# Sixteen gate tiles in pairs, each pair by seven products of 128 tokens, two couples of pairs ahead of two branch groups

## What is computed

```python
    y_a = dsa_attention(aq, ak, av, iq, ik, iw)
    y_b = dilated_attention(bq, bk, bv)
    y_m = memory_attention(mq.reshape(b, s, M_HEADS, M_HEAD_DIM), rmsnorm(mem, g_mem[l]), w_mem_kv[l])
    gates = jax.nn.sigmoid((n @ w_gate[l] + b_gate[l]).astype(jnp.float32)).astype(n.dtype)
    gates = gates.reshape(b, s, N_BRANCHES, d)
    merged = (gates[:, :, 0] * (y_a @ w_branch[l, 0])
              + gates[:, :, 1] * (y_b @ w_branch[l, 1])
              + gates[:, :, 2] * (y_m @ w_branch[l, 2]))
    h = h + merged @ w_out[l]
    h = h + hier_moe(rmsnorm(h, g_ffn[l]), w_group[l], b_group[l], w_sub[l], b_sub[l], w1[l], w3[l], w2[l])
```

## Time and profile before

| what | value |
|---|---|
| time, median of 3 runs | 1039.71 us (1039.53 to 1039.88) |
| profiled execution | 1039.46 us, its span 1037.6 us |
| PE busy | 1012.0 us (98%), 5196 matmul records |
| DVE busy | 445.2 us (43%) |
| ACT busy | 338.8 us (33%) |
| chain that ended last | PE 91%, DVE 4%, DMA 2%, ACT 1% |
| mean granted TensorE clock | 0.998 |

### The profile page before, as it was taken

How to read it: one execution, slowest core, us unless ns; L and a number is a source line. 1 busy time by engine, 2 the same in 40 slices (tenths; PEclk the granted TensorE clock), 3 DMA queues, 4 the chain that set the end, 5 groups by cost and what they waited for, 6 DMA issues and landing times.

```text
span 1037.6 us, 14005 instructions
## 1 busy us (share of the span) xinstructions
PE 1012.0 (98%) x5196; PEld 706.9 (68%) x5196; DVE 445.2 (43%) x1250; ACT 338.8 (33%) x803; POOL 65.2 (6%) x124
## 2 busy tenths in 40 slices
PE   6999999999999999999999999999999999999996
PEld 2468554547887777888888877888888844444442
DVE  5459836456356655355743424831012410000004
ACT  5224134335053247245553134730111411111112
POOL 0060000032100000000000000000000020000000
PEclk9999999999999999999999999999999999999999
DMA  9972125762243331444434342059536799999996
GB/s 362 420 300 84 41 81 197 291 243 81 82 148 136 122 122 63 170 169 151 158 134 155 131 194 81 2 216 422 213 138 227 277 381 422 420 422 419 422 420 253
DMA packets 33936, 227.49 MB, mean 219 GB/s; under 512 B 4577, under 2 KB 4849, under 8 KB 8112
## 3 DMA queue, kind: packets, MB, share of 16 engines
q1 hardware_dynamic: 30784, 214.97, 53.1%
q10 hardware_dynamic: 1920, 9.80, 2.5%
q0 software_dynamic: 1168, 1.85, 0.5%
HBM read 222.15 MB, written 8.41 MB: 222 GB/s over the span
## 4 chain that ended last, share of the span: by engine, by line
PE 91%; DVE 4%; DMA 2%; ACT 1%; issue 1%; SPq 0%; DVEq 0%; ACTq 0%
PE lin L580 21%; PE lin L1189 11%; PE sc L699 6%; PE aux L1189 5%; PE aux L580 5%; PE aux L1076 4%; PE sc L804 4%; PE lin L768 3%; PE aux L834 3%; PE sc L1154 3%; PE lin L820 3%; PE sc L580 3%; PE sc L983 2%; DVE UN L2004 2%; PE lin L596 2%; PE sc L596 2%
## 5 line engine op out<-in xcount | busy, mean ns | idle before, releaser
L580 PE MATMUL lin<-H,ring 128*128 128x256 f32 (+1 forms) x1008 | 222.5, 383 | 0.0
L580 PEld LDWEIGHTS lin<-H,ring 128*128 128x128 f32 x1008 | 191.4, 190 | 29.7 <-issue 4.2
L699 PE MATMUL sc<-H,ring 128*128 128x512 f32 (+1 forms) x192 | 67.3, 496 | 0.0
L2004 DVE SCALAR_TENSOR_TENSOR UN<-UN,cols 128x512 f32<-128x512 f32 (+1 forms) x120 | 66.7, 626 | 0.0
L1406 ACT ACTIVATE SP<-lin 128x512 f32<-128x512 f32 (+2 forms) x88 | 42.1, 486 | 72.1 <-PE lin L820 71.9
L1417 ACT ACTIVATE SP<-SP,ST 128x513 f32<-128x513 f32 (+4 forms) x88 | 53.9, 612 | 6.5 <-DVE ST L1919 6.2
L1916 DVE CUSTOM_DVE_ANT_0 SP<-sc,CW,SK 128x512 f32<-128x512 f32 (+1 forms) x48 | 31.8, 662 | 55.5 <-PE sc L804 55.5
L699 PEld LDWEIGHTS sc<-H,ring 128*128 128x128 f32 x192 | 34.8, 189 | 30.3 <-issue 25.6
L2411 DVE TENSOR_TENSOR PR<-lin,PR 128x512 f32<-128x512 f32 x8 | 5.5, 691 | 94.6 <-PE lin L1189 94.6
L804 PE MATMUL sc<-PR 64*128 64x256 f32 (+3 forms) x240 | 42.2, 434 | 2.9 <-DVE ST L1916 2.1
L1076 PE MATMUL aux<-Y,ring 128*128 128x256 f32 x192 | 42.2, 380 | 0.5 <-DVE Y L1928 0.5
(11 more groups left out here) (428 smaller groups left out, 1541.8 us busy)
## 6 DMA issues: line engine op xcount, KB each, us to landing
ring<-w_stream SPq DMA_DIRECT2D x119, 1024.0 KB, 5.2
SP<-w_stream SPq DMA_DIRECT2D x13, 1024.0 KB, 20.5
UN<-w_stream SPq DMA_DIRECT2D x10, 1024.0 KB, 19.3
PR<-w_stream SPq DMA_DIRECT2D x8, 1024.0 KB, 21.8
CW<-w_stream SPq DMA_DIRECT2D x8, 1024.0 KB, 21.8
X<-w_stream SPq DMA_DIRECT2D x8, 1024.0 KB, 23.8
Y<-w_stream SPq DMA_DIRECT2D x8, 1024.0 KB, 18.1
PR<-ada_in SPq DMA_DIRECT2D x5, 1024.0 KB, 26.8
```

The lines of the kernel that those rows point to most:

```text
L580: m = mm(dst, w[:, k, :], rhs(k), start=n == 0, stop=n == KT - 1)
L699: m = mm(bank[:, 0:ns * SEQ], filling["w"][:, k, :], H[:, 0:ns, k, :], start=k == 0, stop=k == KT - 1)
L2004: ins = v.scalar_tensor_tensor(out=CV[:, t, 0:ns, :], in0=u, scalar=w, in1=CV[:, t, 0:ns, :], op0=ALU.mult, op1=ALU.add)
```

## The change

The sixteen gate tiles that are made after the attention (8 to 23) are taken in eight pairs, two pairs are a couple (`GATES_LATE`), and the four couples go in twos: couples 0 and 1 ahead of branch groups `mp` 0 and 1, couples 2 and 3 ahead of `mp` 2 and 3. A pair is one ring unit `w` (two tiles, each split into two halves of the contraction, `lo` and `hi`). The tokens are split into two halves of 128 and the contraction into two halves; the product is made with seven products of four matmuls with 128 tokens. VectorE makes three sums of the weights beside one sum in place, and four sums of the tokens once. ScalarE copies partial results out of the bank between products that add to the same bank, VectorE adds the rest, and ScalarE then applies the sigmoid in SBUF. `MORE` and half of `X1` hold the weight sums, so SyncE loads nine expert units instead of eleven at the end of the attention, and four instead of two after the last branch product. The stream's order is changed to match, with the one block of padding moved behind the early gates.

```diff
+        G_S = [MORE[:, 512 * q:512 * (q + 1)] for q in range(4)] + [X1[:, 1024:1536], X1[:, 1536:2048]]
+        G_T = NB.rearrange("p (q k n) -> p q k n", q=4, k=4)
+        def gate_unit(c, x):
+
+            return FIRST_GATE + 2 * c + x + 3 * (c // 2)
...
+            def paired_gates(c):
...
+                for x in range(2):
...
+                    w[x] = unit_of_pair()
...
+                    if c:
+                        pe.wait_ge(quarter_added, g_added(c - 1, x, 3))
...
+                    quarter(g_banks(c, x)[0], w[x][:, 0, lo], h11).then_inc(quarter_made, 1)
+                for x in range(2):
+                    quarter(g_banks(c, x)[1], w[x][:, 0, hi], h21).then_inc(quarter_made, 1)
+                for x in range(2):
+                    pe.wait_ge(quarter_read, g_read(c, x, 1))
+                    pe.wait_ge(tokens_mixed, G_TOKENS + 3)
+                    pe.wait_ge(weights_mixed, G_WEIGHTS + 8 * c + 3 * (x + 1))
+                    quarter(g_banks(c, x)[0], G_S[x][1], t2, start=False).then_inc(quarter_made, 1)
...
             attention("abm", early_gate)
+            at["block"] += at["block"] % UNIT
+            turn["prefetch"] = at["block"] // UNIT + SLOTS
             for mp in range(4):
-                for n in range(max(EARLY, 6 * mp), 6 * mp + 6):
-                    gate(*divmod(n, 3))
+                if mp % 2 == 0:
+                    paired_gates(mp)
+                    paired_gates(mp + 1)
                 if mp == 0:
-                    turn["prefetch"] = at["block"] // UNIT + SLOTS
                     attended("abm")
...
-            for n in range(RING_AT - 2):
+            for n in range(RING_AT - 4):
                 sp.dma_start(ASIDE[n], w_stream[BASE + n].rearrange("p b n -> p (b n)")).then_inc(aside_in[n], 16)
...
-            for n in (RING_AT - 2, RING_AT - 1):
+            for n in range(RING_AT - 4, RING_AT):
                 load_expert(BASE + n, n)
...
+            def mixed_gate(c, x):
+
+                u, (lo, hi) = gate_unit(c, x), LO_HI
+                w, (s1, s2, s4) = ring[:, u % SLOTS, :, :], G_S[x]
+                dve.wait_ge(unit_in[u % SLOTS], 16 * (u // SLOTS + 1))
+                if c:
+                    dve.wait_ge(quarter_made, g_at(c - 1, x, 5))
+                v.tensor_tensor(s1, w[:, 1, lo], w[:, 1, hi], ALU.add).then_inc(weights_mixed, 1)
+                v.tensor_tensor(w[:, 1, lo], w[:, 0, lo], w[:, 1, lo], ALU.subtract).then_inc(weights_mixed, 1)
+                dve.wait_ge(weights_mixed, G_WEIGHTS + 8 * c + 3 * x + 1)
+                v.tensor_tensor(s2, s1, w[:, 0, lo], ALU.subtract).then_inc(weights_mixed, 1)
...
+            def mixed_first(p):
+
+                if p in (12, 14):
+                    mixed_gate(0, (p - 12) // 2)
+                elif p == 16:
+                    mixed_gate_last(0)
+
+            def joined_gates(c, then):
...
+                for x in range(2):
+                    to = halves_of(pairs[x][1])[1]
+                    dve.wait_ge(quarter_read, g_read(c, x, 7))
+                    v.tensor_tensor(to, to, G_Z[:, x, :], ALU.add).then_inc(quarter_added, 1)
+                    if x < len(then):
+                        mixed_gate(then[x], x)
+                for x in range(2):
...
+                    v.tensor_tensor(to, to, g_banks(c, x)[2], ALU.add).then_inc(quarter_added, 1)
+                if len(then) == 2:
+                    mixed_gate_last(then[0])
 
-            attention("abm")
+            attention("abm", mixed_first)
 
             for mp in range(4):
+                if mp % 2 == 0:
+                    joined_gates(mp, (mp + 1, mp + 1))
+                    joined_gates(mp + 1, () if mp else (2,))
                 for b in range(3):
...
+                if mp == 0:
+                    mixed_gate(2, 1)
+                    mixed_gate_last(2)
```

More of the change, by code:

```diff
@@ L101 @@
 FIRST_OUT = (4 + len(FIRST1) + sum(n if what == "gate" else 4 * n for what, _, _, n in SEQUENCE if what == "ada") + GATES) // 2
+FIRST_GATE = (4 + 14 + 4 * 8 + 6 + 2 * (KT + 2) + IN1 + IN2 + EARLY + 1) // 2
 FIRST_V = (4 + 14 + 4 * 8 + 6 + 2 * (KT + 2) + IN1 + BV) // 2
@@ L1050, in _ @@
             pe.wait_ge(idx_mask, 1)
-            def gate(t, b):
-                bank = lin_bank(("gate", t, b))
-                product(bank[:, 0:SEQ], lambda k: H[:, 0, k, :]).then_inc(lin_ready, 1)
+            def paired_gates(c):
+                lo, hi = LO_HI
+                h11, h12 = H[:, 0, 0:4, 0:P], H[:, 0, 0:4, P:SEQ]
+                h21, h22 = H[:, 0, 4:8, 0:P], H[:, 0, 4:8, P:SEQ]
+                t1, t3, t2, t4 = (G_T[:, q, :, :] for q in range(4))
+                w = {}
+                for x in range(2):
+                    assert at["block"] // UNIT == gate_unit(c, x)
+                    w[x] = unit_of_pair()
+                    if c == 0 and x == 0:
+                        pe.wait_ge(scores_taken, scored_first["abm"] + len(STAGES["abm"]))
+                        pe.wait_ge(fill_taken, GATES_FROM + EARLY)
+                        pe.wait_ge(lin_taken, at["lin"])
+                    if c:
+                        pe.wait_ge(quarter_added, g_added(c - 1, x, 3))
+                    if c >= 2:
+                        pe.wait_ge(quarter_read, g_read(c - 2, x, 4))
+                    quarter(g_banks(c, x)[0], w[x][:, 0, lo], h11).then_inc(quarter_made, 1)
[8 more added lines that the diff above has]
+                    if c:
+                        pe.wait_ge(quarter_read, g_read(c - 1, x, 4))
+                    quarter(g_banks(c, x)[2], G_S[x][0], t1).then_inc(quarter_made, 1)
+                for x in range(2):
+                    pe.wait_ge(quarter_read, g_read(c, x, 6))
+                    quarter(g_banks(c, x)[0], w[x][:, 1, lo], t3, start=False).then_inc(quarter_made, 1)
+                for x in range(2):
+                    pe.wait_ge(quarter_read, g_read(c, x, 5))
+                    pe.wait_ge(weights_mixed, G_WEIGHTS + 8 * c + 7 + x)
+                    quarter(g_banks(c, x)[2], G_S[x][2], h22, start=False).then_inc(quarter_made, 1)
+                for x in range(2):
+                    pe.wait_ge(quarter_read, g_read(c, x, 7))
+                    pe.wait_ge(tokens_mixed, G_TOKENS + 4)
+                    quarter(g_banks(c, x)[0], w[x][:, 1, hi], t4, start=False).then_inc(quarter_made, 1)
+                at["owed"] += 2
@@ L2197, in _ @@
                     v.tensor_tensor(BVT[:, 0, f1], BVT[:, 0, f1], gamma, ALU.add).then_inc(quarter_added, 1)
+                    if g == 1:
+                        g1, g3, g2, g4 = (G_T[:, q, :, :] for q in range(4))
+                        h11, h12, h21, h22 = (H[:, 0, k:k + 4, a:a + P] for k in (0, 4) for a in (0, P))
+                        v.tensor_tensor(g1, h12, h11, ALU.subtract).then_inc(tokens_mixed, 1)
+                        v.tensor_tensor(g3, h22, h12, ALU.subtract).then_inc(tokens_mixed, 1)
+                        dve.wait_ge(tokens_mixed, G_TOKENS + 1)
+                        v.tensor_tensor(g2, h22, g1, ALU.subtract).then_inc(tokens_mixed, 1)
+                        dve.wait_ge(tokens_mixed, G_TOKENS + 3)
+                        v.tensor_tensor(g4, h21, g2, ALU.subtract).then_inc(tokens_mixed, 1)
                 if t == BQ - 1:
@@ new lines, in mixed_gate_last @@
+            def mixed_gate_last(c):
+                for x in range(2):
+                    w, (s1, s2, s4) = ring[:, gate_unit(c, x) % SLOTS, :, :], G_S[x]
+                    dve.wait_ge(weights_mixed, G_WEIGHTS + 8 * c + 3 * x + 3)
+                    if c:
+                        dve.wait_ge(quarter_made, g_at(c - 1, x, 3))
+                    v.tensor_tensor(s4, w[:, 0, LO_HI[1]], s2, ALU.subtract).then_inc(weights_mixed, 1)
+            def mixed_first(p):
[3 more added lines that the diff above has]
+                    mixed_gate_last(0)
@@ L2236, in _ @@
+            attention("abm", mixed_first)
             for mp in range(4):
+                if mp % 2 == 0:
+                    joined_gates(mp, (mp + 1, mp + 1))
+                    joined_gates(mp + 1, () if mp else (2,))
                 for b in range(3):
                     for t in (2 * mp, 2 * mp + 1):
[L2239 to L2242, removed]
+                        dve.wait_ge(gates_in, 3 * t + b + 1)
@@ L2525 @@
     branches = [pairs_of(a["w_branch_2"][0, b][grouped] if b == 0 else a["w_branch_2"][0, b]) for b in range(3)]
+    stream += [gates[n % 3 * KT + n // 3][None] for n in range(EARLY)]
+    stream.append(np.zeros((PADDED - N_HEAD_BLOCKS, P, KT * P), np.float32))
     for mp in range(4):
-        stream += [gates[n % 3 * KT + n // 3][None] for n in (range(max(6 * mp, EARLY), 6 * mp + 6) if mp else range(EARLY))]
+        if mp % 2 == 0:
+            stream += [gates[n % 3 * KT + n // 3][None] for pairs in GATES_LATE[mp:mp + 2] for pair in pairs for n in pair]
         stream += [branches[b][mp][None] for b in range(3)]
     stream.append(tiles_of(a["w_out_2"][0], KT))
```

(1 more changed line is left out.)

73 lines of the change are left out of this document (64 added, 9 removed).

## The result

The changed kernel takes 1050.59 us (median of 4 runs, 1048.42 to 1053.43), the kernel before beside it 1039.62 us (4 runs, 1039.47 to 1039.88): a ratio of 1.0106, 95% interval 1.0093 to 1.0119. The forecast was 1052.2 us and slower.

The account below looks back on a forecast made before the run. The prediction took TensorE alone to set the pace in the gates and branches; its terms summed to +12.5 us on the profiled 1039.46 us, 1052.0, and 1052.2 us for the median, range 1046.5 to 1056.0.

Parts of the forecast that it names:

- quarter products: Late gates on TensorE: four couples of shorter matmuls take 50.1 us instead of 55.25, −5.1 us.
- wait for the attention's last copy: End of attention: couple 0 needs no attention result, so it covers TensorE's 0.52 us wait, −0.5 us.
- sums in the attention: Attention steps 12, 14, 16: VectorE's weight sums delay TensorE's scores, +3.3 us, bounds nothing and 5.4.
- couple 0 to 1: Before couple 1: VectorE's sums free the bank late, +1.0 us, bounds 0 and 2; the same between couples 2 and 3.
- unit behind the expert loads: First branch group: VectorE waits for couple 2's first unit, twelfth on the queue; TensorE waits +7.8 us, bounds 0 and 10.4.
- clock: First branch group after the 7.8 us wait: products run at a lowered clock, +2.5 us, bounds nothing and 6.9.
- after the first branch group: Start of second group: VectorE's merge and couple 2's other sums make TensorE wait, +2.5 us, bounds 1 and 3.5.
- Rival 2: The unit behind the expert loads lands early, out of queue order: 1041.9 us, chance 6%.
- Rival 1: The sums in the attention are absorbed in VectorE's idle time: 1048.9 us, chance 8%.
- rival 4: More waits inside the couples, each of four losing another 1 us: 1056 us, chance 7%.
- Rival 5: Weight loads not hidden at 128 columns, 448 records taking 136 us instead of 50: about 1138 us, chance 1%.
- Rival 3: VectorE is never late, so TensorE never waits for a sum and only its own terms stay: 1034.1 us, chance 4%.

Follow-up runs that it names:

- the later four of the same kernel: The changed kernel run again with nothing edited: 1049.62 us, median of 4 runs, ratio 1.0091.
- The run with the sums moved: Couple 0's eight weight sums moved from attention steps 12, 14 and 16 to 20 to 22, against the changed kernel: 1048.16 us, ratio 1.0079.
- the runs with five and seven units: Changed kernel, but only five or seven of the nine expert units issued ahead of the ring's next two: 1041.25 us (five), 1043.95 us (seven).
- 1047.72 us without any fall: Changed kernel plus unread extra TensorE products, 28 in the first branch group's stop and 8 in the second's: 1047.72 us, median of four runs.
- one stop filled: Changed kernel plus 28 unread extra TensorE products in the first branch group's stop: 1048.46 us, median of 4 runs.
- the last experiment: Changed kernel with five units ahead, couple 0's sums moved, couple 2's five sums spread, product 3 added ahead of weight sums: 1033.49 us, ratio 0.994.
- the four edits: Five expert units ahead, couple 0's sums moved, couple 2's five sums spread, product 3 added earlier, against the changed kernel: 1033.49 us, ratio 0.994.

## Why the prediction was right, and where it was off

The mechanisms held one by one, and the direction with them. The size is off: the sum gives 1052.0 us for the profiled execution, and that execution took 1048.42. That the forecast lies only 1.6 us above the median of the first four runs is partly luck, since these four range over 5 us and the later four of the same kernel have their median 2.6 us below the forecast. By its own terms, in us, for the profiled execution (0.23 is the restart behind a stop):

| term | predicted | measured | from |
|---|---|---|---|
| quarter products | −5.1 | −5.2 | four couples of 12.51 (748.24 to 760.75) against 55.25 |
| wait for the attention's last copy | −0.5 | −0.8 | 0.52, and 10.63 against 10.36 |
| sums in the attention | +3.3 | +2.3 | 690.29 against 688.0 |
| couple 0 to 1 | +1.0 | +0.6 | 0.33 and 0.23 |
| unit behind the expert loads | +7.8 | +7.8 | 7.57 and 0.23 |
| clock | +2.5 | +1.5 | 8.60 − 7.14 |
| after the first branch group | +2.5 | +2.4 | 2.16 and 0.23 |
| couple 2 to 3 | +1.0 | +0.5 | 0.29 and 0.23 |
| sum | +12.5 | +9.0 | 794.50 − 785.46 = 9.0 |

- **The sums in the attention** and the clock were the terms that were sized worst, each 1.0 too high. For the sums the step was "2.0 us put behind the copy of step 12 reach the scores of pair 14 as 1.6 us". The three sums delay the next read by 1.80 us (657.98 to 659.78), and TensorE stood for 1.22, so the slack was near 0.6 us and not 0.4. The third stop of 0.1 never came. The run with the sums moved gives back 2.3.
- **Between couples** I reckoned VectorE over at T + 13.5; it was over at T + 12.9 (702.70 + 0.48, T = 690.29), because three sums take 1.8 us in a row and the small ones less than 0.25.
- **The unit** landed at T + 33.7, forecast T + 34.0, and TensorE resumed at T + 36.6, forecast 37.3. The step that gave this, eleven units ahead at 2.5 us each, is the one that the runs with five and seven units confirm. Rival 2 (the unit comes out of queue order) fell with them.
- **The clock** is right as a median and for a partly wrong reason. Against 1047.72 us without any fall, the first four runs lose 2.9 us (1050.59; 3.4 when each kernel is set against the kernel before beside it) and the later four 1.9 (1049.62); I took 2.5, and the profiled execution lost 1.5. But I tied it to the long wait alone. The runs with five and seven units ahead and with one stop filled show that it also falls behind the stop of 2.16 us, in some executions.
- **Rival 1** (sums absorbed) and **rival 4** (more waits inside the couples) don't hold: the stops are there, and inside the couples no TensorE record waits. **Rival 5** doesn't either: the 112 records of a couple pass in 12.51 us, 0.112 each. **Rival 3** did not hold for this kernel, yet its time, 1034.1 us, is what the last experiment reaches by taking each stop away: 1033.49.

## What to carry to other kernels

A product made cheaper for the bound engine is worth its saving only if the helper's extra work finds idle time and its loads stand early enough in the queue: here the saving of 6.0 us was real, and the four edits that cost no computation turned a loss of 1.1% into a gain of 0.6%. When a list of one engine gains a wait for a load, count what stands ahead of that load on its queue, and look at what is queued behind the wait: here a multiplication that needed nothing of the load. Put several sums one by one between the instructions that the bound engine waits for, not in a block ahead of them.

## What was not expected of the hardware

- The granted clock fell to 1.2 GHz behind stops of 2.16 us in some executions and not in others, and, there and behind the stop of 2.97 us with seven units ahead, 0.3 to 1.4 us after the work had resumed (at 740.98 behind a restart at 739.99 in the kernel with one stop filled, windows below). What decides whether it falls behind the short stop stays open. In the stop of 7.4 to 7.8 us it fell in each of the four traces that have it, while TensorE still stood, and came back only 2.9 to 5.5 us after the restart.

```profile
737.90:739.90 2.00, 0.00 (x0) 0.00 (x0) 2.00 (x5) 0.00 (x0) 0.00 (x0) 1.00 0.00 0
740.00:740.90 0.90, 0.90 (x4) 0.82 (x5) 0.18 (x1) 0.00 (x0) 0.00 (x0) 1.00 0.00 0
741.10:744.30 3.20, 3.20 (x9) 2.45 (x9) 0.42 (x1) 0.00 (x0) 0.00 (x0) 0.50 0.81 261
```

- What the fall costs is half the time that work overlaps it: 1.46 us for 2.9 us (8.60 − 7.14), 2.17 for 4.3 in the second profile of the changed kernel (9.31 − 7.14).
- After a stop of TensorE the next 16 records take 0.23 us longer in the chain (2.02 against 1.79 us), even after a stop of 0.3 us. Most of it is lost overlap: without a stop the next record starts 0.16 us before the one before it ends (691.91 against 690.12 + 1.95 in couple 0).
